# Layer 1's ranges shifted by one position, Silu by way of tanh, exponentials put together, and weight chunks of 512 rows by 512 columns

## What is computed

```python
for l in range(2):
    h = _rmsnorm(x, norm1_g[l])
    z = h @ w_in[l]                                   # u, v, lru_x, lru_gate, gate_A, gate_B
    y_a = _gmlp_branch(u, v, ...)                     # gelu(u) * (mix of 128 positions of layernorm(gelu(v)))
    xc = conv_b + sum(conv_w[k] * lru_x at t-1+k, k = 0..3)
    h_lru = forward scan(xc) + backward scan(xc)      # h_t = a_t h_(t-1) + sqrt(1 - a_t^2) * i_t * xc_t
    y_b = h_lru * gelu(lru_gate)                      # a_t = exp(-8 r_t softplus(-lambda)), r, i = sigmoid(...)
    x = x + (sigmoid(gate_A) * y_a + sigmoid(gate_B) * y_b) @ w_out[l]
    h = _rmsnorm(x, norm2_g[l])
    ff = silu(h @ w_ffn_in[l][:, :D_FF]) * (h @ w_ffn_in[l][:, D_FF:])
    x = x + ff @ w_ffn_out[l]
return _rmsnorm(x, final_g)
```

## Time and profile before

| | |
|---|---|
| three runs, slowest core | 4383.49 us median (4165.4 to 4581.22) |
| the profiled execution | 4155.68 us, span of its slowest core 4154.1 us |
| spans of the eight cores | 4102.2 to 4154.1 us |
| mean granted TensorE clock, slowest core | 0.954 of full speed |
| bytes read and written in device memory | 748.27 MB and 206.57 MB |

### The profile page before, as it was taken

The page is one execution under the profiler, slowest core; times in us unless marked ns, Lnnn a source line. Parts: engine busy times, 40 slices in busy tenths (PEclk is TensorE's granted clock), DMA queues, the critical chain, the costliest instruction groups (busy, mean ns, idle before and its releaser), DMA issues.

```text
span 4154.1 us, 56145 instructions; the slowest of 8 cores (4102.2 to 4154.1 us)
## 1 busy us (share of the span) xinstructions
PE 3728.3 (90%) x17874; PEld 1695.4 (41%) x17874; DVE 2239.0 (54%) x3267; ACT 2524.1 (61%) x3492; POOL 344.5 (8%) x595
## 2 busy tenths in 40 slices
PE   5778778698999989999998999977999999999988
PEld 2333333243444444444443444433444444444443
DVE  4777777634365655646565462765365444444322
ACT  5777878662558485765847672886384644735211
POOL 2111110000010000001000000000000000000000
PEclk9989989898999999999999999988999999999999
DMA  9877887687979879697987665674676576674653
GB/s 198 147 150 147 156 146 167 225 183 235 208 241 221 256 216 234 203 243 225 222 257 213 198 215 182 223 230 144 205 233 221 199 240 209 202 248 153 200 162 105
DMA packets 354911, 836.90 MB, mean 201 GB/s; under 512 B 35184, under 2 KB 159296, under 8 KB 340416
## 3 DMA queue, kind: packets, MB, share of 16 engines
q1 hardware_dynamic: 238880, 767.24, 59.1%
q0 software_dynamic: 115744, 66.07, 14.5%
HBM read 748.27 MB, written 206.57 MB: 230 GB/s over the span
## 4 chain that ended last, share of the span: by engine, by line
PE 71%; DMA 10%; ACT 8%; issue 6%; DVE 4%; POOL 1%; SPq 0%; ACTq 0%; DVEq 0%; POOLq 0%
PE pfall L1160 28%; PE pfall L980 15%; PE pfall L1179 14%; PE pfall L1136 4%; PE pfall L962 3%; PE pfall L702 2%; PE pfall L932 2%; DMA xs<-x 2%; DMA hf<-HF 2%; PE pfall L1215 2%; DMA YA<-guth 2%; DMA xm<-XC 1%; DMA wzx<-w_in 1%; ACT guth L982 1%; DMA xr<-XL 1%
## 5 line engine op out<-in xcount | busy, mean ns | idle before, releaser
L1160 PE MATMUL pfall<-hTa,wr 128*128 128x512 bf16 x2816 | 633.5, 384 | 34.8 <-ACT sg L1165 25.3
L1160 PE MATMUL pfall<-hTb,wr 128*128 128x512 bf16 x2816 | 622.7, 382 | 4.9 <-ACT hTb L1150 2.7
L1179 PE MATMUL pfall<-wr,ff 128*128 128x512 bf16 x2816 | 610.6, 379 | 0.9 <-ACT sg3b L1165 0.9
L980 PE MATMUL pfall<-hTa,wr 128*128 128x512 bf16 x1920 | 431.0, 381 | 12.5 <-ACT guth L982 9.8
L1160 PEld LDWEIGHTS pfall<-hTa,wr 128*128 128x128 bf16 x2816 | 276.1, 99 | 373.6 <-issue 55.3
L1160 PEld LDWEIGHTS pfall<-hTb,wr 128*128 128x128 bf16 x2816 | 276.2, 98 | 342.4 <-issue 13.8
L1179 PEld LDWEIGHTS pfall<-wr,ff 128*128 128x128 bf16 x2816 | 275.0, 98 | 333.9 <-issue 1.4
L1136 PE MATMUL pfall<-wr,mT 128*128 128x512 bf16 x1024 | 245.4, 399 | 71.0 <-DVE mT L1125 50.5
L889 DVE SCALAR_TENSOR_TENSOR xm<-zb,cols,xm 128x512 f32<-128x512 f32 x384 | 277.1, 746 | 25.6 <-ACT hz L939 11.0
L1184 DVE TENSOR_TENSOR xr<-pfall,xr 128x512 f32<-128x512 f32 x128 | 80.3, 684 | 386.8 <-PE pfall L1179 386.2
L980 PEld LDWEIGHTS pfall<-hTa,wr 128*128 128x128 bf16 x1920 | 186.1, 98 | 233.8 <-issue 17.5
(11 more groups left out here) (150 smaller groups left out, 5287.1 us busy)
## 6 DMA issues: line engine op xcount, KB each, us to landing
wr<-WB SPq DMA_DIRECT2D x832, 512.0 KB, 5.5
XC<-xm SPq DMA_DIRECT2D x32, 1024.0 KB, 9.1
YA<-guth SPq DMA_DIRECT2D x128, 256.0 KB, 5.0
HF<-ib SPq DMA_DIRECT2D x32, 1024.0 KB, 11.6
xm<-XC SPq DMA_DIRECT2D x32, 1024.0 KB, 7.8
ya<-YA SPq DMA_DIRECT2D x128, 256.0 KB, 7.3
hf<-HF SPq DMA_DIRECT2D x128, 256.0 KB, 6.6
WB<-w_ffn_in POOLq DMA_DIRECT2D x44, 512.0 KB, 25.1
```

The lines of the kernel that those rows point to most:

```text
L980: op = sc.mm(key, p, [(lambda e, k=k: e.matmul(p.f(), lhsT=w(k), rhs=hT[:, k, lo:lo + TT], start=(k == 0), stop=(k == KC - 1)), bh + [bw]) ...
L1160: op = sc.mm(keyf(t), p, [(lambda e, k=k, o=o, q=q, p=p: e.matmul(p.f(), lhsT=q[:, k, o:o + 128], rhs=hT[:, k, 0:TT], start=(k == 0), stop ...
L1179: sc.mm(keyf(nb, q, s), ps[s], [(lambda e, f=f, s=s, t=t, q=q, p=ps[s]: e.matmul(p.f(), lhsT=fs[f][0][:, s * 128:(s + 1) * 128], rhs=t[:, ...
```

## The change

Five things are changed at once.

1. **Ranges.** In layer 1 the convolution's outputs of tile j are now those of positions 512 j + 1 to 512 j + 512. Nothing of the tile before is needed, so the layer-1 part runs one turn later only (`ja = j + 1`), the loop has NT + 1 = 9 turns, and one buffer `h1` takes the place of two. The outputs go to `XC1` and the backward scan's to `HB1`, both 4608 positions long in one piece; stage 3 loads its 512 positions from there, starting one element before a multiple of 512. Position 0 is computed by itself (`first_column`) in the last turn. In this last turn the gates R1 stand among the V groups.
2. **Silu.** Silu(x) is x (1 + tanh(x/2)) / 2: ScalarE computes tanh, VectorE multiplies (1 + tanh) with the PSUM bank (one instruction more for each of 2 x 8 x 22 = 352 blocks), and the half is put into the addition after FO.
3. **Exponentials.** `after=` holds the first four of a recurrence back, in the order that is made at build, until the gate of block 3 stands, and the last four until that of block 7.
4. **Weight chunks** of all names but "fo" are 512 rows by 512 columns; a block needs two of them, and two serve four blocks. "fi" has 24 chunks, where it had 22. The resident weights of stage 1 are loaded in the same pieces.
5. **Stage 3, tile 0:** the gates of tile 2 stand between FO's groups, not behind them. The casts of layer 1's weights go out as 16 in turn 0 and 8 in turn 1, where they were 12 and 12.

The core of the diff:

```diff
+    XC1 = scratch("XC1", [128, KC, S + TT], F32)
+    HB1 = scratch("HB1", [128, KC, S + TT], F32)
...
+    def wload(name, addr, src, order=range(4), into=None):
+
+        r = into if into is not None else {}
+        for i in order:
+            nb, kh = divmod(i, 2)
+            ap, b = T(f"{name}{i}", [128, 4, 512], BF16, addr + i * 4 * K)
+            castload(ap, [b], src[kh * 512:(kh + 1) * 512, nb * 512:(nb + 1) * 512].rearrange("(k p) n -> p k n", p=128),
...
+                     128 * 8 * K)
+            r[i] = (ap, b)
...
+            gk.append(key + (t,))
...
-                0.81, reads=[bra[c], bhcneg], writes=[bra[c]], tset="exp")
+                0.81, reads=[bra[c], bhcneg], writes=[bra[c]], tset="exp", after=gk[-9] if c < 4 else gk[-1])
...
-            sl = slice(None, None, 1 if d == 0 else -1)
-            sc.op("dve", lambda e, c=c, sl=sl: e.tensor_tensor_scan(
-                out=ib[:, c, sl], data0=ra[:, c, sl], data1=ib[:, c, sl],
+            rv = lambda t, c: t[:, c, 0:n] if d == 0 else t[:, c, 0:n][:, ::-1]
+            sc.op("dve", lambda e, c=c, rv=rv: e.tensor_tensor_scan(
+                out=rv(ib, c), data0=rv(ra, c), data1=rv(ib, c),
                 initial=(0.0 if first else pcar[:, c:c + 1]), op0=ALU.mult, op1=ALU.add), 1.27,
...
-            elif name == "fi":
-                for q in range(FC // 2):
-                    for half in range(2):
-                        c0 = half * DFF + q * 256
-                        lst.append((w[:, c0:c0 + 256].rearrange("(k p) n -> p k n", p=128), KC))
             else:
-                for i in range(4):
-                    lst.append((w[:, i * 256:(i + 1) * 256].rearrange("(k p) n -> p k n", p=128), KC))
+
+                blocks = [i * 512 for i in range(2)]
+                if name == "fi":
+                    blocks = [half * DFF + q * 512 for q in range(6) for half in range(2)]
+                for i, c0 in enumerate(blocks):
+                    n = 512 if i < 10 else DFF - 5 * 512
+                    for kh in range(2):
+                        lst.append((w[kh * 512:(kh + 1) * 512, c0:c0 + n].rearrange("(k p) n -> p k n", p=128), 4))
             for i, (src, n) in enumerate(lst):
...
+    def xcstore1(j, xm, h):
+        t0 = (j + 1) * TT
+        sc.dma("sp", lambda e: e.dma_start(out=XC1[:, 4 * h:4 * h + 4, t0:t0 + TT], in_=xm.group(h)),
+               XHALF, reads=[xm[4 * h + i][1] for i in range(4)], writes=[bXC1[j + 1][h]])
+
+    def xcload1(j, xm, h):
+        sc.dma("sp", lambda e: e.dma_start(out=xm.group(h), in_=XC1[:, 4 * h:4 * h + 4, (j + 1) * TT - 1:(j + 2) * TT - 1]),
+               XHALF, reads=[bXC1[j][h], bXC1[j + 1][h]], writes=[xm[4 * h + i][1] for i in range(4)])
+
+    def hbstore(j):
+        t0 = (j + 1) * TT
+        for h in range(2):
+            sc.dma("sp", lambda e, h=h: e.dma_start(out=HB1[:, 4 * h:4 * h + 4, t0:t0 + TT], in_=ib[:, 4 * h:4 * h + 4, :]),
+                   XHALF, reads=bib[4 * h:4 * h + 4], writes=[bHB1[j + 1][h]])
+
...
-        def block(self, c):
-
-            t, b = self.chunk(c // 2)
-            o = c % 2 * 128
-            return (lambda k: t[:, k, o:o + 128]), b
+        def block(self, c, sub=0, subs=1):
+
+            i = 2 * (c // 4 * subs + sub)
+            a = [self.chunk(i), self.chunk(i + 1)]
+            o = c % 4 * 128
+            return (lambda k: a[k // 4][0][:, k % 4, o:o + 128]), (lambda k: a[k // 4][1])
 
...
-        sc.op("act", lambda e: e.activation(out=sg, in_=ps[0].f(), func=AF.Silu), 0.62, writes=[bsg],
-              psum=[ps[0]], tset="silu")
+        sc.op("act", lambda e: e.activation(out=sg, in_=ps[0].f(), func=AF.Tanh, scale=0.5), 0.62, writes=[bsg],
+              psum=[ps[0]], tset="tanh")
+        sc.op("dve", lambda e: e.scalar_tensor_tensor(
+            out=sg, in0=sg, scalar=1.0, in1=ps[0].f(), op0=ALU.add, op1=ALU.mult), 0.74, reads=[bsg], writes=[bsg],
+            psum=[ps[0]])
...
-                sc.op("dve", lambda e, nb=nb, p=ps[s], xr=xr: e.tensor_add(
-                    out=xr[:, nb * 512:(nb + 1) * 512], in0=p.f(), in1=xr[:, nb * 512:(nb + 1) * 512]), 0.7,
+                sc.op("dve", lambda e, nb=nb, p=ps[s], xr=xr: e.scalar_tensor_tensor(
+                    out=xr[:, nb * 512:(nb + 1) * 512], in0=p.f(), scalar=0.5, in1=xr[:, nb * 512:(nb + 1) * 512],
+                    op0=ALU.mult, op1=ALU.add), 0.74,
                     reads=[bxr], writes=[bxr], psum=[ps[s]])
...
-        if j == NT - 1:
-            ph = P("t")
-            sc.mm(keyh, ph, [(lambda e, k=k: e.matmul(
-                ph.f(0, 2), lhsT=w(k), rhs=hT[:, k, TT:TT + 2], start=(k == 0), stop=(k == KC - 1)),
-                [bh[NS - 1], bw]) for k in range(KC)], 0.065)
-            sc.op("dve", lambda e: e.tensor_copy(out=z[:, c, 0:1], in_=ph.f(1, 2)), 0.2, writes=[bz[c]], psum=[ph])
         p = P("main")
...
+    def first_column(key):
+
+        cols, bcols = cols2[1]
+        hbias, bhbias = hbias2[1]
+        hcneg, bhcneg = hcneg2[1]
+        z, bz = hz1[-1]
+        v = lambda i: lone[:, i, :]
+        dv = lambda fn, reads=(): sc.op("dve", fn, 0.17, reads=[blone] + list(reads), writes=[blone])
+        dv(lambda e: e.tensor_mul(out=v(0), in0=z[:, :, 0], in1=cols[:, 8:16]), bz + [bcols])
+        for k in (1, 2):
+            dv(lambda e, k=k: e.tensor_mul(out=v(1), in0=z[:, :, k], in1=cols[:, 8 + 8 * k:16 + 8 * k]), bz + [bcols])
+            dv(lambda e: e.tensor_add(out=v(0), in0=v(0), in1=v(1)))
+        dv(lambda e: e.tensor_add(out=v(0), in0=v(0), in1=cols[:, 32:40]), [bcols])
+        sc.dma("sp", lambda e: e.dma_start(out=XC1[:, :, TT - 1:TT], in_=lone[:, 0:1, :].rearrange("p o c -> p c o"),
+                                                allow_slow_non_contiguous=True), 4096,
+               reads=[blone], writes=bXC1[0])
+        sc.op("dve", lambda e: e.tensor_copy(out=lonb, in_=v(0)), 0.17, reads=[blone], writes=[blonb])
+        p = P("gate")
...
+              reads=[blone, b_quart], writes=[blone], tset="sqrt")
+        dv(lambda e: e.scalar_tensor_tensor(out=v(6), in0=v(3), scalar=1.0, in1=v(0), op0=ALU.add, op1=ALU.mult))
+        dv(lambda e: e.tensor_mul(out=v(6), in0=v(6), in1=v(5)))
+        ca, bca = car1[0]
+        dv(lambda e: e.tensor_mul(out=v(7), in0=v(4), in1=ca), [bca])
+        dv(lambda e: e.tensor_add(out=v(7), in0=v(7), in1=v(6)))
+        sc.dma("sp", lambda e: e.dma_start(out=HB1[:, :, TT - 1:TT], in_=lone[:, 7:8, :].rearrange("p o c -> p c o"),
+                                                allow_slow_non_contiguous=True), 4096,
...
-        for s in (3, 0, 1, 2):
+        hT, bh = hT1
+        for s in range(NS):
...
-    T1AT = {1: 3, 3: 0, 5: 1, 6: 2}
-    ZAT = {3: [0], 4: [1], 5: [2], 6: [3, 4], 7: [5, 6, 7]}
+    T1AT = {1: 0, 2: 1, 3: 2, 4: 3}
+    ZAT = {4: [0], 5: [1, 2], 6: [3, 4], 7: [5, 6, 7]}
     xtp = None
-    for i in range(NT + 2):
+    for i in range(NT + 1):
         j = NT - 1 - i
         g = G2 + i
-        ja = j + 2 if j + 2 < NT else None
+        ja = j + 1 if j + 1 < NT else None
         tok = []
         for c in range(KC):
...
+            if j < 0:
+
+                a = [t for t in a if t[0] != "R1"]
+                for n, c in enumerate(range(KC)):
+                    a.insert(2 + n + n // 2, ("R1", c))
...
-                cast_next(2 if i < 2 and f % 6 == 0 else 1, op)
+                cast_next(2 if i == 0 else 1, op)
...
-            tok += [("R", c) for c in range(KC)]
+            for c in range(KC):
+                tok.insert(tok.index(("FO", c // 6, c % 6, NS - 1)) + 1, ("R", c))
```

155 lines of the change are left out of this document (72 added, 83 removed).

## The result

The changed kernel is slower than the kernel before: 1.0164 times its time, with a 95% interval of 1.0108 to 1.022; whether it is slower by 2% stays open. Its profiled execution took 4236.5 us (span 4234.9) against 4155.7 (span 4154.1), 81 us more where 90 less were forecast. Some executions, whatever the kernel, ran longer on one or both halves of the chip at a lower granted clock; comparisons use the others, and profiles are read on a core that was not disturbed.

What follows compares the result with a forecast made beforehand. TensorE, busy 90% of the span, was taken as the bound, so only its standstill could be won. Terms 64 - 46 + 46 + 5 + 3 + 14 + 4 = 90 us took 4155.7 to 4066; 8-in-10 range 4010 to 4130.

Steps and rivals of the forecast that it cites:

- the part on tables: Full turns of stage 2: table switches fall from 35 to 15, which with the shorter waits wins 10.7 us a turn.
- 0 elsewhere: Weight chunks: the larger ones win 3 us at the start and change nothing in the rest of the kernel.
- Cost 0: Feed-forward parts: VectorE's 352 added instructions, 263 us in all, find room and cost no time.
- rival C: Feed-forward parts: VectorE frees PSUM banks late; gain gone at 4156, slower at 4240 or more; chance 0.10, half of it slower.
- Turn 1: Stage 2: turn 1 takes over turn 9's work, becomes a full turn and costs 46 us more.
- the last stretch: From stage 2's last FO to stage 3's first FI: one turn less, 264 us becomes 200, 64 won.
- stage 3's tile 0: Stage 3: gates placed among FO's groups, and tile 1's G and B not waiting for that scan, win 14 us.
- Z's wait for the transpose: Each turn: the Z group behind the fourth transpose reads its copy at once, costing 1.4 us.
- the `vg` wait: Full turns: TensorE's 3.7 us wait for `vg` goes away, as two Gelus now go first on ScalarE.
- rival B: Turns 1 to 7: norm, transposes and Z in one chain, 7 us of wait each, 49 us in all: 4115; chance 0.09.
- The 7 us forecast up to the end of turn 0: Larger weight chunks win 3 us at the start, and fewer table switches in FI win 4 in turn 0.
- Rival A: FI of full turns: transfers set the pace, XM8's load no earlier or held by four-chunk bursts; about 4110; chance 0.22.

Runs made afterwards that it cites:

- small chunks: The changed kernel with weight chunks put back to 1024 rows by 256 columns; profiled execution 4125.2 us, no ratio.
- late gates: The changed kernel with layer 0's gate steps among FI at int(11 + 1.4 c), not int(7 + 1.7 c); ratio 0.9949 to the kernel before.
- shift alone: The changed kernel with Silu, exponentials not held and chunks of 256 columns, keeping the shifted ranges and stage 3's gates among FO; ratio 0.9953 to the kernel before.

## Why the prediction was wrong

*The step that failed* is in the part on tables. It costed only what ScalarE's saved time removes, and said: "What is late next is still the load of XM8 ... and, at OP, `mT`." What is late next is the store of layer 1's states, which the earlier trace rows do not show because ScalarE came to the gate just behind its landing (0.5 us in turn 4). It also took for granted that what is stored and loaded lands as before, and the store lands 8.2 us later there. In five full turns this turned -46 us into +50: FI +11.9 a turn (8.0 of it TensorE's standstill, 37.9 to 77.8 us in five; with the rest goes a mean granted clock of 0.92 in FI against 0.98), the part from OP to FI -2.1, the merge about equal.

*Weight chunks, "0 elsewhere".* With nothing else changed, the small chunks are worth some 80 to 110 us; with late gates, the ratio moves from 0.9949 to 0.984, some 45 us. The prediction asked whether four chunks come in time for TensorE and said yes; at OP they do not (10.6 us of waits in five turns), and small chunks save 4.5 us a turn between OP and FI on the mean of the cores. It did not ask who stands behind them: the `HB1` store, which lands after 26.5 us with large chunks and 15.9 with small ones. How much of these 10.6 us is the size of the groups, and how much the changed order and the later issue, stays open.

*VectorE, "Cost 0".* It was never the bound, and stage 3 had no wait for `ff`, so rival C fell. Yet the product of the tanh form made VectorE a link: held by ScalarE, it held `guth` and, through the YA store, `ff`. 22.3 of TensorE's 77.8 us in five FI are waits for `ff`, and with Silu TensorE has none. What the product costs hangs on the rest: 2.3% in the changed kernel, 1.5% without the hold and with small chunks (1.0105 with it, 0.9953 with Silu, and the intervals do not meet), and nothing that shows with small chunks, the hold and late gates. So "Cost 0" holds only in the last of these orders.

*Turn 1* was taken as a full turn. It is one plus 10 us in the changed kernel, plus 25 with the shift alone. Of the 30 us beyond the forecast 20 are the longer full turn and 10 its own: waits of 5.4 us for `hz`, 4.2 for `mT` and 2.3 for `guth`, as far as rows show. The earlier trace rows gave a sign of it: turn 1 lost 27 us, a full turn 19.

*Right or nearly:* the last stretch, 207 us for 200 (in the shift-alone kernel 199.9), the largest term; stage 3's tile 0, 147.7 us from FI to OP for a forecast 147; Z's wait for the transpose, 1.5 us for 1.4; the `vg` wait gone; the merge before Z in time (rival B fell); table loads 219 in the profile for "about 240". In this profile stage 3's other tiles lost 8 us (tiles 2 and 3 take 167 and not 163; TensorE's wait for `xr` is 23.9 us where it was 14.4), which was not forecast; on the mean of the eight cores stage 3 gained 8.6 us of the 14. The 7 us forecast up to the end of turn 0 did not come: 964.7 us against 957.8 on that mean.

*Rival A* named the place, FI's transfers with the DMA share at 0.98, and the four-chunk bursts, but the wrong transfer, and priced it at 3 us of a win instead of 9, never at a loss. The sign was missed because every mechanism on the list but C was a gain that shrinks; no rival was a buffer still being read. C's 4240 is close to the result by accident: its mechanism did not happen.

## What to carry over

When an engine is made faster, list for each instruction in its queue not only what it needs but whose bytes it overwrites, and when the last reader of those will be done: a store counts as a reader until it has landed, not until it has been issued. An engine's slowness can be what hides such a wait; the time from a store's landing to the next writer, read from the trace (0.5 us here in turn 4, of 18.3 from its issue), is the slack that a speed-up may spend, and a change in what goes ahead of the store spends it too. And parts that each look like a loss, by what undoing them alone brings, can be one collision in the main: moving the instruction that collides was worth about as much as undoing any of them.

## What the hardware showed that was not expected

The store of 1 MB to `HB1` lands 12.9 to 28.1 us after its issue (medians of the kernels that were tried). With groups of two chunks it was 15.9 us and with groups of four 26.5, but with four and an issue 6 us earlier 18.3: no single edit here explains it. Over an FI the 16 DMA engines are busy 0.86 to 1.02 of the time, but move only 196 to 242 GB/s, while the merge moves 282 at 0.97: a share near 1 is not a measure of what is moved. And a lower granted clock went with the standstills. FI of turn 4, with waits of 11.5 and 4.7 us, was granted 0.92 and had TensorE busy 84.6 us; the same FI in the kernel before, granted 1.00, took 80.3 us of work: to 16 us of standing still came 4 of slower work.
